# Gate columns in one product, part of the query projection among the modulation tiles, and an expert tile loaded earlier

## The reference, cut to what matters

```python
mod = jax.nn.silu(c) @ w_ada[l] + b_ada[l]            # 6 x 1024: shift, scale, gate, twice
h = modulate(x, norm1_g[l], sh1, sc1)                  # rms_norm(x) * (1 + scale) + shift
proj = h @ w_in[l]                                     # q, k, v of attention, qk/v/o of the mLSTM, 8 gate columns
...                                                    # attention and mLSTM, then
x = x + g1[:, None, :] * (jnp.concatenate([attn, hm], axis=-1) @ w_out[l])
h2 = modulate(x, norm2_g[l], sh2, sc2)
x = x + g2[:, None, :] * hier_moe(h2, ...)             # 32 experts, top 2 of a group
```

## Time and profile before

| what | value |
|---|---|
| median of 3 runs | 1475.91 us (1473.51 to 1476.65) |
| profiled execution | 1474.02 us, its span 1472.2 us |
| mean granted clock of TensorE in it | 0.973 of full speed |
| PE busy | 1362.4 us, 93% of the span |
| DMA | 388.22 MB, mean 264 GB/s |

### The profile page before, as it was taken

How to read it: one execution, slowest core, us unless ns; L and a number is a source line. 1 busy time by engine, 2 the same in 40 slices (tenths; PEclk the granted TensorE clock), 3 DMA queues, 4 the chain that set the end, 5 groups by cost and what they waited for, 6 DMA issues and landing times. The chain is left out here.

```text
span 1472.2 us, 24368 instructions
## 1 busy us (share of the span) xinstructions
PE 1362.4 (93%) x10107; PEld 1024.5 (70%) x10107; DVE 652.9 (44%) x1236; ACT 264.1 (18%) x573; POOL 228.5 (16%) x227
## 2 busy tenths in 40 slices
PE   5999999998788986978899999999999999999998
PEld 2476546665556653645478688888887877788887
DVE  2545542100100110101624336384399999986563
ACT  2313121110100110101120031100333333320000
POOL 0000100000000000000547530298121221000000
PEclk9999999999989997999999999999999999999999
DMA  9855769999999999999634343466653444334440
GB/s 399 325 229 216 303 268 407 425 425 427 424 426 426 426 425 424 425 428 410 241 119 167 115 154 132 155 216 227 221 191 135 152 146 152 130 128 158 170 169 34
DMA packets 50827, 388.22 MB, mean 264 GB/s; under 512 B 6288, under 2 KB 21392, under 8 KB 29088
## 3 DMA queue, kind: packets, MB, share of 16 engines
q1 hardware_dynamic: 48128, 381.35, 65.0%
q10 hardware_dynamic: 2592, 5.31, 1.0%
HBM read 379.76 MB, written 6.88 MB: 263 GB/s over the span
## 5 line engine op out<-in xcount | busy, mean ns | idle before, releaser
L1490 DVE TENSOR_TENSOR ada_part<-ada_part,ps 64x256 f32<-64x256 f32 x32 | 13.5, 423 | 417.6 <-ACT ada_part L1445 417.6
L2589 PE MATMUL ps<-hT,ring 128*128 128x256 f32 x768 | 170.6, 382 | 1.0 <-PEq L2029 1.0
L2589 PEld LDWEIGHTS ps<-hT,ring 128*128 128x128 f32 x768 | 146.2, 192 | 20.5 <-issue 1.4
L1558 POOL TENSOR_SCALAR end_stat<-end_ss 128x1 f32<-128x1 f32 x2 | 0.9, 472 | 491.7 <-ACT expert L1548 491.6
L1358 PE MATMUL ps<-memT,hT 128*128 128x256 f32 x192 | 50.9, 425 | 21.0 <-DMA hT<-in_mem_quarters 20.3
L1445 ACT ACTIVATE ada_part<-ps 64x256 f32<-64x256 f32 x32 | 12.1, 377 | 323.7 <-PE ps L1395 323.7
L267 PE MATMUL ps<-ring,hT 128*128 128x512 f32 x160 | 69.8, 594 | 0.0
L1061 PEld LDWEIGHTS ps<-sel,tokens 128*128 128x128 f32 x544 | 62.0, 192 | 8.1 <-issue 8.1
L1878 PE MATMUL ps<-ring,zT 128*128 128x256 f32 x288 | 66.9, 380 | 0.0
L1061 PE MATMUL ps<-sel,tokens 128*128 128x64 f32 x544 | 64.3, 277 | 0.7 <-DVE sel L1070 0.7
L1358 PEld LDWEIGHTS ps<-memT,hT 128*128 128x128 f32 x192 | 40.2, 215 | 29.5 <-DMA hT<-in_mem_quarters 22.1
(11 more groups left out here) (653 smaller groups left out, 2533.7 us busy)
## 6 DMA issues: line engine op xcount, KB each, us to landing
ring<-in_weights SPq DMA_DIRECT2D x69, 2048.0 KB, 7.9
expert<-in_experts SPq DMA_DIRECT2D x36, 2048.0 KB, 24.1
ring<-in_experts SPq DMA_DIRECT2D x35, 2048.0 KB, 23.6
expert_room<-in_experts SPq DMA_DIRECT2D x12, 2048.0 KB, 23.4
late_room<-in_experts SPq DMA_DIRECT2D x12, 2048.0 KB, 25.6
hT<-in_mem_quarters SPq DMA_DIRECT2D x20, 512.0 KB, 23.8
s_c_bar<-c_bar_out ACTq DMA_DIRECT2D x16, 256.0 KB, 2.7
c_bar<-s_c_bar SPq DMA_DIRECT2D x16, 256.0 KB, 2.7
```

The lines of the kernel that those rows point to most:

```text
L1490: dve.tensor_tensor(act_s, gate, h_ps[w3_out, :], ALU.mult).then_inc(act_ready, 1)
L2589: last = pe.matmul(out[:, f, :], w[:, kk, (2 * h + f) * P:(2 * h + f + 1) * P], k.hT[:, kk, :], start=(kk == 0), stop=(kk == KD - 1))
```

## The change

Five edits go together.

1. The gate weights are laid out as 36 columns (0 to 3 and 32 to 35 filled, zeros between), so that one product per chunk takes the place of two. The array is 144 KB in place of 32 KB and lies in the router's weight tensor `w_router`, so the router's weights are issued only when the gate product is done.
2. The ring's first five tiles are issued as A0, A2, Q, A1, A3 with slots 0, 2 (Q), 1: `slot_of` and `landing_of` take the place of n % 3. From A0's and A2's ends hang the issues of A1 and A3.
3. The first half of Q (256 tokens x 512 columns are 16 products) is spread: eight of its products, on chunks 0 to 3 of `hT`, are put among the modulation tiles A1 and A3, with accumulators in PSUM banks 4 and 5; the other eight follow the gate product. ACT takes Q from those banks (`take_q`).
4. `late_room` exists from the start; `mix_room0` and `mix_room1` are parts of it, and what used them late moves away (`mixT` into `hT`, `cst` into `mem_tile`, `sq` into the second half of `expert0[2]`, the residual's products into `o_m`, for which DVE waits for `x1_summed`).
5. Expert tile 7 is therefore issued during `stage_mix`, behind tile VM and a wait for the fourth score product (`scored`), and not at the start of `stage_experts`.

```diff
+def slot_of(n):
+    return (0, 1, 0, 1, 2)[n] if n < N_EARLY_SLOT else (n + 1) % RING
...
-                for n in range(RING + 1):
-                    tile(n)
+                for p in ("A0", "A2", "Q", "A1", "A3"):
+                    tile(TILE_OF[p])
                 sp.dma_start(w_gate[:], d["w_gate"]).then_inc(wg_in, 16)
                 sp.dma_start(pos[:], d["positions"]).then_inc(pos_in, 16)
-                tile(4)
+                tile(TILE_OF["K"])
                 sp.dma_start(k.mix_const[:], d["mix_consts"]).then_inc(mix_const_in, 16)
                 sp.dma_start(mem, d["mem"]).then_inc(mem_in, 16)
-                tile(5)
+                tile(TILE_OF["V"])
                 sp.dma_start(k.const[:, N_FIRST_CONST:], d["consts"][:, N_FIRST_CONST:]).then_inc(late_const_in, 16)
-                tile(6)
...
+                sp.wait_ge(*banks.full("GT"))
                 sp.dma_start(a["w_router"][:], d["w_router"]).then_inc(a["w_router_in"], 16)
...
+                    if n == TILE_OF["VM"]:
+                        sp.wait_ge(scored, 4)
+                        load_expert_tile(k, sp, a, 7)
...
-                for m in (1, 3):
-                    ada_tile(k, banks, pe, m, crep)
-                    ada_columns(k, banks, pe, m, part)
+                pe.wait_ge(hT_ready, 1)
+                k.wait_tile(pe, TILE_OF["Q"])
+                q_half(0, range(4))
+                ada_tile(k, banks, pe, 1, crep)
+                q_half(1, range(2))
+                ada_columns(k, banks, pe, 1, part)
+                ada_tile(k, banks, pe, 3, crep)
+                q_half(1, range(2, 3))
+                ada_columns(k, banks, pe, 3, part)
+                q_half(1, range(3, 4))
...
                 for kk in range(KD):
-                    for g in range(2):
-                        last = pe.matmul(banks.bank("GT")[32 * g:32 * g + 4, 0:TOK], w_gate[:, kk, 4 * g:4 * g + 4],
-                                         k.hT[:, kk, :], start=(kk == 0), stop=(kk == KD - 1), skip_group_check=True)
+                    last = pe.matmul(banks.bank("GT")[0:36, 0:TOK], w_gate[:, kk, :], k.hT[:, kk, :],
+                                     start=(kk == 0), stop=(kk == KD - 1))
                 last.then_inc(banks.done("GT"), 1)
-                half("Q0")
-                half("Q1")
+                q_half(0, range(4, KD)).then_inc(q_done, 1)
+                q_half(1, range(4, KD)).then_inc(k.tile_done, 1)
                 half("K0")
                 pe.wait_ge(mem_scaled, TT)
...
     def sync(sp):
         load_expert_tile(k, sp, a, 5)
-        load_expert_tile(k, sp, a, 7)
```

More of the change, by code:

```diff
@@ L36, with landing_of @@
 TILE_OF = {name: n for n, name in enumerate(FRONT)}
+N_EARLY_SLOT = 5
+def slot_of(n):
+    return (0, 1, 0, 1, 2)[n] if n < N_EARLY_SLOT else (n + 1) % RING
+def landing_of(n):
+    outside = TILE_OF["M2"]
+    return sum(slot_of(m) == slot_of(n) for m in range(n + 1) if m != outside)
 N_OUT, N_EXP = 2, 32
@@ L143, in slot @@
     def slot(self, n, k=8):
-        return self.ring[:, n % RING, :].rearrange("p (k n) -> p k n", k=k)
+        return self.ring[:, slot_of(n), :].rearrange("p (k n) -> p k n", k=k)
     def wait_tile(self, pe, n):
-        outside = TILE_OF["M2"]
-        pe.wait_ge(self.landed[n % RING], 16 * (n // RING + 1 - int(n > outside and n % RING == outside % RING)))
+        pe.wait_ge(self.landed[slot_of(n)], 16 * landing_of(n))
 def bc(ap, axis, n):
@@ L318, in stage_mix @@
         sb = lambda n, s, dt=F32: k.sb(n, s, dt, ctx=ctx)
-        r1, r2 = (sb(f"mix_room{i}", [P, 2048]) for i in range(2))
+        r1, r2 = (a["late_room"][:, 2048 * i:2048 * i + 2048] for i in range(2))
         r3, r4 = (a["expert0"][2][:, 2048 * i:2048 * i + 2048] for i in range(2))
@@ L341, in stage_mix @@
         qkT = r2[:].rearrange("p (f t) -> p f t", f=KD)
-        mixT, cst = qkT, r2[:, 1024:1540].rearrange("p (h e) -> p h e", h=4)
+        mixT, cst = k.hT, a["mem_tile"][:, 3104:3620].rearrange("p (h e) -> p h e", h=4)
         memn, mem = tokens(r3), tokens(r4)
@@ L368, in stage_mix @@
          o_part, gcol_ready, ops_out, x1_added, x1_summed, x1_rstd_ready, x1_scaled, x1_turned,
-         h_by_dve, h_by_act, gain_ready) = (k.sem(n) for n in names)
+         h_by_dve, h_by_act, gain_ready, q_done, q_out) = (k.sem(n) for n in names)
         fm = lambda b0, n: k.ps[:, b0:b0 + n, :].rearrange("p b (f t) -> p (b f) t", f=2)
@@ L429, in _, with q_half @@
                 ada_columns(k, banks, pe, 2, part)
-                for m in (1, 3):
-                    ada_tile(k, banks, pe, m, crep)
-                    ada_columns(k, banks, pe, m, part)
+                def q_half(t, kks):
+                    w = k.slot(TILE_OF["Q"])
+                    for kk in kks:
+                        last = pe.matmul(k.ps[:, 4 + t, :], k.hT[:, kk, t * P:(t + 1) * P], w[:, kk, :],
+                                         start=(kk == 0), stop=(kk == KD - 1))
+                    return last
+                pe.wait_ge(hT_ready, 1)
[8 more added lines that the diff above has]
+                q_half(1, range(3, 4))
                 pe.wait_ge(hT_ready, 3)
@@ L448, in _ @@
                 pe.wait_ge(m_ready, 1)
+                pe.wait_ge(q_out, 2)
                 for t in range(TT):
@@ L634, in _, with take_q @@
                 act.activation(tmp, tmp, ACT.Ln, bias=1.0).then_inc(f_exp, 1)
-                take("Q0", qk[:, 0, 0:512])
+                def take_q(t):
+                    act.wait_ge(*((q_done, 1) if t == 0 else (k.tile_done, TILE_OF["Q"] + 1)))
+                    act.activation(qk[:, t, 0:512], k.ps[:, 4 + t, :], ACT.Copy).then_inc(q_out, 1)
+                take_q(0)
                 act.wait_ge(m_ready, 1)
@@ L643, in _ @@
                     act.activation(memn[:, t, :], mem[:, t, :], ACT.Square, accum_out=ss_m[:, t:t + 1]).then_inc(mem_summed, 1)
-                take("Q1", qk[:, 1, 0:512])
+                take_q(1)
                 take("K0", qk[:, 0, 512:1024])
@@ L695, in _ @@
                         act.wait_ge(x1_added, 2 * t + n + 1)
-                        act.activation(sq[:, t, c], k.x[:, t, c], ACT.Square, scale=D ** -0.5,
+                        act.activation(o_m[:, n, :], k.x[:, t, c], ACT.Square, scale=D ** -0.5,
                                        accum_out=ss_1[:, t, n:n + 1]).then_inc(x1_summed, 1)
@@ L988, in add_out @@
                         dve.wait_ge(k.tile_done, TILE_OF[f"O{n}"] + 1)
+                        dve.wait_ge(x1_summed, n + 1)
                     c = slice(n * 512, (n + 1) * 512)
-                    dve.tensor_tensor(sq[:, t, c], k.ps[:, 2 * n + t, :], k.row("b_g1")[:, c], ALU.mult)
+                    dve.tensor_tensor(o_m[:, n, :], k.ps[:, 2 * n + t, :], k.row("b_g1")[:, c], ALU.mult)
                     dve.drain()
-                    dve.tensor_tensor(k.x[:, t, c], k.x[:, t, c], sq[:, t, c], ALU.add).then_inc(x1_added, 1)
+                    dve.tensor_tensor(k.x[:, t, c], k.x[:, t, c], o_m[:, n, :], ALU.add).then_inc(x1_added, 1)
                 def scale_x(t):
@@ L1328, in _ @@
                     sp.wait_ge(done, n_pass * N_TILE + (last + 1 - N_TILE + DONE0))
-                    sp.dma_start(k.ring[:, n % RING, :], k.dram["weights"][n]).then_inc(k.landed[n % RING], 16)
+                    sp.dma_start(k.ring[:, slot_of(n), :], k.dram["weights"][n]).then_inc(k.landed[slot_of(n)], 16)
             @block.tensor
@@ L2546, in load_tile @@
                     sp.wait_ge(k.tile_done, T_S5_SCAN + m - (RING - 1))
-                    sp.dma_start(k.ring[:, (T_S5_SCAN + m) % RING, :], k.dram["weights"][T_S5_SCAN + m]
-                                 ).then_inc(k.landed[(T_S5_SCAN + m) % RING], 16)
+                    sp.dma_start(k.ring[:, slot_of(T_S5_SCAN + m), :], k.dram["weights"][T_S5_SCAN + m]
+                                 ).then_inc(k.landed[slot_of(T_S5_SCAN + m)], 16)
                 load_b(0)
```

35 lines of the change are left out of this document (20 added, 15 removed).

## The result

The changed kernel takes 1482.53 us (1478.24 to 1491.82, 10 runs), the kernel before took 1475.93 on the same chip (1473.51 to 1482.5, 10 runs). The ratio is 1.0049, with an interval from 1.0028 to 1.007: between 4.1 and 10.3 us **slower**. The same kernel measured again with twelve runs gave 1.0035 [1.0014, 1.0056]. The profiled execution took 1480.24 us with a span of 1478.5, which is 6.2 more than the profiled execution of before.

A forecast was written before the change was run, and what follows sets the result against it. Transfers were taken to bound the experts' stage and TensorE everything else. A turn 1.2 us later plus 1.7 for the clock gave +2.9 on 1475.91, so 1478.8 us, with 8 in 10 from 1473.4 to 1481.8.

The forecast's parts named there:

- Gates: Gate products: 8 of 256 columns take 3.5 us instead of 5.18; the 1.7 are the clock's, the form gives nothing.
- Query products: Eight Q products, 7.0 us, leave the stretch behind the gates; TensorE is ready to turn the memory rows at 54.5.
- What comes late: `mix_const` lands at 39.4 instead of 34.1; TensorE waits 3.9 us and turns the memory rows 1.2 us later.
- its upper bound: If A1 ends after 28.8, K's issue is late, the queue runs empty behind A3: 1.5 us or so more.
- The clock behind the wait: Granted clock falls after TensorE's new wait for the memory rows: 1.7 us, bounds 0 and 3.4.
- Tile 7 and the rest: Issuing expert tile 7 early costs 0, bounded by 5.0 us; the delayed OM tile, router weights and moved buffers cost 0.
- that rival: Experts' stream gains tile 7's 5.0 us from the transfer-bound stretch: -2.1, 1473.8 us; chance 0.09.
- the first rival: Memory rows are in time at the turn, so TensorE keeps its 2.7 us: 1473.2 us; chance 0.14.
- The first Q products run at half clock: Rival: four Q products before A1 cost up to 3.4 us more, constants up to 1.9 later: +4.8, 1480.7; chance 0.15.
- the sum: Whole kernel: 1.2 us for the later turn plus 1.7 for the clock behind the wait, +2.9 us.

The follow-up runs named there:

- old_gates: The changed kernel with the gates as two products of 4 columns per chunk again, from the same 36-column array: 1483.16 us, 1.0037 of the kernel before.
- late_const: The changed kernel with the old order of tiles and Q products, and `mix_const` and memory rows issued behind K's tile: 1476.74 us, 0.9998 of the kernel before.
- again: The changed kernel unaltered, measured again beside other follow-up kernels: 1484.6 us, 1.0035 of the kernel before.
- t7_late: The changed kernel with expert tile 7 issued at the head of the experts' stage again: 1485.83 us, 1.0047 of the kernel before.
- mix_fill: The changed kernel with constants and memory rows issued ahead of K's tile, plus three unused products before Q's first products: 1476.31 us, 0.9986 of the kernel before.
- mix_first: The changed kernel with `mix_const` and the memory rows issued ahead of K's tile: 1477.22 us, 0.9996 of the kernel before.
- no_q: The changed kernel with the old order of tiles and Q products, 36 gate columns and early tile 7 kept: 1477.54 us, 0.9999 of the kernel before.
- turn_k1: The changed kernel with the turn of the memory rows moved behind K1: 1480.22 us, 1.0008 of the kernel before.

## Why the prediction was wrong

The direction was right and the size was not: +2.9 us were forecast, +6.6 measured, above the range's end of 1481.8.

**Gates.** Right: 3.64 us for 3.5, by `old_gates` nothing from the form itself, and by `late_const` (5.16) the 1.7 were the clock's. The Trainium skill ("TensorE: Matmul & The Clock Gate", Part 3) says that products at different tile positions run concurrently; the runs agree, 3.62 against 3.64.

**Query products.** The 7.0 us did leave the stretch (7.13 behind the gates), and the waits for tiles did go. TensorE was ready at 56.6, not 54.5: 0.4 from `hT`'s later chunks, 1.9 from the clock on the four products, less 0.2 elsewhere.

**What comes late.** Right in kind. The constants were at DVE at 40.28, not 39.4. By the forecast's reckoning the bytes in front allowed 39.4, but K's issue came at 31.11 and not at 28.8 and the queue stood empty. The text had that as its upper bound, with 1.5 us; it cost 0.9. TensorE's own 2.1 cost nothing more, since it would have stood there anyway: it waited 2.70 and not 3.9. The turn started 2.1 later than before, not 1.2.

**The clock behind the wait.** 1.7 were taken, 1.64 measured in the first profile, and 2.6 in `again`, where the wait was 4.16.

**Tile 7 and the rest.** Right at 0 (`t7_late`, and 9.09 us in three profiles). The experts' stage was no tile shorter, so that rival fell. The memory rows weren't in time, so the first rival fell as well.

**The step that failed** is "The first Q products run at half clock", held for a rival with a chance of 0.15 and left out of the sum. It happened in all eight profiles that keep that wait of 2.50 us (5.40 in six, 6.62 and 6.74 in two), and it doesn't compete with the forecast but adds to it. The words for it were in the text (single columns just before, an empty stretch). Its price of +1.9 is what `mix_fill` shows against `mix_first`, where the constants don't hold the chain. In the changed kernel they do, and in the first profile after it came to 0.9: the constants at 40.28 and not 39.4. So K1 stands 3.75 later there, 2.1 and 1.64, where the sum had 2.9; the gather 4.0; the stage's end 4.6, of which no run takes the last 0.8 apart. With the whole +1.9 the sum is +4.8, within the measured 4.1 to 10.3.

**What the sum took from one execution.** Four profiles have the changed order with nothing remedied. K1 ends 3.7 later than before in `old_gates`, 3.75 in the first profile after, 5.8 in `t7_late` and 8.5 in `again`: 5.4 on average, an estimate from four executions. Two things make them differ. The landing of the constants took 8.7 us from the issue in the first two and 10.2 in the others, so the wait was 4.2 and the half clock reached into K1. And `again` had the slow start, which put 2.3 us on the issue of `mix_const`. Eight of the fourteen profiles of this case had a slow start. In the old order the landings behind it take most of it up (0.3 on the constants in `no_q`), in the new one A1, K's issue, `mix_const` and the turn hang in a row on when TensorE gets there. Two of the four also had a gather 3.1 or 3.2 us slower. How these shares stand in the timed runs isn't shown, since those have no timeline. Slow starts by themselves don't explain the scatter: it is 1474.6 to 1492.1 for the changed kernel and 1473.6 to 1480.7 for `no_q`, but also just 1473.6 to 1481.7 for `mix_first`, whose front hangs on TensorE's start all the same. The slowest runs of the changed kernel (1491.7, 1491.8 and 1492.1) show a mean granted clock of 0.966 or 0.967, where its fastest show 0.976 and 0.977, so part of their time is more half clock somewhere.

**Open.** Why the experts' gather took 6.75 to 6.96 us in three profiles (`again`, `turn_k1`, `t7_late`) and 3.75 or 3.76 in the other eleven, all behind a wait of 0.66 to 0.67. All three have the new order with the constants behind K, and ran in the first group, but four of the eleven have that order too and `no_q` ran in that group. These 3.1 us are part of why `again` is slower than `mix_first`, and no run here takes them apart. Why the landing takes between 8.7 us and 10.2 in the seven profiles with that order is open as well, and so is why A2's product is slow in some.

## What to carry to other kernels

Before a tile is moved ahead on a queue, follow what is issued behind it and what its issue hangs on. A transfer whose issue waits for an engine inherits the delays of that engine (here 2.3 us in K's issue, 31.11 for 28.8), and a small one that others wait for (here 592 KB of constants) belongs ahead of the tile that has to wait. Filling a wait for a landing with work is a gain only if the new wait in front of that work is cheap: where TensorE stood for 2.5 us or more behind single columns, or ahead of turning rows, the half clock was a term of the sum, not a risk beside it. Then ask which chain that term lies on: the same fall cost 1.9 us where TensorE was the last to come and 0.9 where the constants were. And a wait for a landing that looks like loss in one profile may be what absorbs a slow start in others, so look at several executions before it is taken out.

## What the hardware showed unexpectedly

- Before the turn, waits of 2.70, 2.75, 2.75, 4.16 and 4.22 us were all followed by half clock (3.43 to 3.68 for the turn); waits of 1.02, 1.82 and 1.83 by none (1.97). The length of the wait doesn't decide it by itself. The gates behind 1.60 took 5.18 before and 5.16 in `late_const`, but 3.64 in `no_q`; a group at 174 to 183 us behind 1.06 or 1.07 took 8.83 in six profiles and 7.13 in eight; and at 722 to 735 us the same tile stood behind 2.53 or 2.54 us in every kernel, and took 7.10 or 7.11 in seven executions and 8.54 to 8.80 in the other seven.
- The start isn't the same in all executions: A2's product took 1.92 us in six profiles and 3.4 to 3.64 in eight, though the granted clock reads 1.00 over it in either case.
- Two issues exchanged in their order, with the same bytes and the same work, were worth 6 to 8 us (0.9996 against 1.0035 and 1.0049), uncertain by 3 to 4.
